# Layer 0 of a hybrid decoder step: the exponential's series and S5's input tables move from DVE to POOL, and POOL's larger memsets move behind its loads

## What is computed

```python
proj = jnp.einsum('btd,de->bte', x, w_in)
o_hg, s_hg_new = _chunked_gated_linear(...)      # HGRN2
o_rt, s_rt_new = _chunked_gated_linear(...)      # retention
y5, s_re_new, s_im_new = _s5_scan(su, s5_log_dt, s5_a_re, s5_a_im, s5_b_re, s5_b_im, ...)
mixed = jnp.concatenate([o_hg, o_rt, y5], axis=-1) @ w_out
x = _layer_norm(ALPHA * x + mixed, ln1_w, ln1_b)
ff = jnp.square(jax.nn.relu(x @ w_up)) @ w_down
x = _layer_norm(ALPHA * x + ff, ln2_w, ln2_b)
```

## Time and profile before

| | |
|---|---|
| median of 3 runs | 835.95 us (834.85 to 836.22) |
| the profiled execution | 836.35 us |
| its span, first to last instruction | 834.6 us |
| PE busy | 749.3 us (90%), 7662 matmuls |
| DVE busy | 577.6 us (69%), 1056 instructions |
| ACT busy | 416.0 us (50%), 760 instructions |
| POOL busy | 36.0 us (4%), 44 instructions |
| mean granted PE clock | 0.948 of 2.4 GHz |

### The profile page before, as it was taken

How to read it: one execution, slowest core, us unless ns; L and a number is a source line. 1 busy time by engine, 2 the same in 40 slices (tenths; PEclk the granted TensorE clock), 3 DMA queues, 4 the chain that set the end, 5 groups by cost and what they waited for, 6 DMA issues and landing times. The chain is left out here.

```text
span 834.6 us, 18462 instructions
## 1 busy us (share of the span) xinstructions
PE 749.3 (90%) x7662; PEld 711.0 (85%) x7662; DVE 577.6 (69%) x1056; ACT 416.0 (50%) x760; POOL 36.0 (4%) x44
## 2 busy tenths in 40 slices
PE   4779678988999999989997989799899999999994
PEld 4669667788999999989986988587799999999993
DVE  7997995445778899885445789834577886666443
ACT  4726131444577755446345624444466874455323
POOL 4000010210000000000010002010000000000000
PEclk9989886998999999999996999899899999999998
DMA  8442111352435455444441333413144555555521
GB/s 330 150 143 85 53 53 50 114 203 74 141 123 179 167 177 192 159 145 142 173 152 51 102 104 105 143 51 110 55 173 139 184 172 187 178 177 178 179 99 53
DMA packets 30580, 113.61 MB, mean 136 GB/s; under 512 B 3521, under 2 KB 3729, under 8 KB 29985
## 3 DMA queue, kind: packets, MB, share of 16 engines
q1 hardware_dynamic: 27936, 101.83, 36.6%
q0 software_dynamic: 1984, 9.52, 3.0%
q10 hardware_dynamic: 576, 1.08, 0.3%
HBM read 108.24 MB, written 4.18 MB: 135 GB/s over the span
## 5 line engine op out<-in xcount | busy, mean ns | idle before, releaser
L1436 DVE TENSOR_TENSOR w_low<-w_raw,w_high 128x1024 fp32r<-128x1024 f32 x192 | 236.5, 1232 | 152.3 <-ACT w_high L1014 149.6
L1014 ACT ACTIVATE w_high<-w_raw 128x1024 fp32r<-128x1024 f32 x192 | 202.5, 1055 | 242.6 <-PE stream L963 231.5
L961 PE MATMUL stream<-a_high,w_high 128*128 128x264 f32 x768 | 237.9, 310 | 33.7 <-DVE a_low L1441 21.7
L962 PE MATMUL stream<-a_low,w_high 128*128 128x264 f32 x768 | 229.2, 298 | 0.0
L963 PE MATMUL stream<-a_high,w_low 128*128 128x264 f32 x768 | 228.4, 297 | 0.0
L961 PEld LDWEIGHTS stream<-a_high,w_high 128*128 128x128 f32 x768 | 155.8, 203 | 44.3 <-issue 22.4
L962 PEld LDWEIGHTS stream<-a_low,w_high 128*128 128x128 f32 x768 | 156.3, 204 | 0.3
L963 PEld LDWEIGHTS stream<-a_high,w_low 128*128 128x128 f32 x768 | 155.7, 203 | 0.0
L961 PE MATMUL stream<-h_high,w_high 128*128 128x264 f32 x512 | 148.6, 290 | 1.2 <-issue 0.5
L962 PE MATMUL stream<-h_low,w_high 128*128 128x264 f32 x512 | 145.1, 283 | 0.0
L963 PE MATMUL stream<-h_high,w_low 128*128 128x264 f32 x512 | 145.0, 283 | 0.0
(11 more groups left out here) (369 smaller groups left out, 953.7 us busy)
## 6 DMA issues: line engine op xcount, KB each, us to landing
w_raw<-in_weights SPq DMA_DIRECT2D x192, 512.0 KB, 3.3
mats<-in_matrices POOLq DMA_DIRECT2D x2, 1024.0 KB, 5.5
S_hg<-in_state_hg POOLq DMA_DIRECT2D x2, 768.0 KB, 5.0
out_hg_s<-S_hg POOLq DMA_DIRECT2D x2, 768.0 KB, 3.7
consts<-in_constants POOLq DMA_DIRECT2D x1, 1484.5 KB, 9.2
X<-in_xT ACTq DMA_DIRECT2D x4, 264.0 KB, 5.7
out_y<-X SPq DMA_DIRECT2D x1, 1056.0 KB, 3.9
S_rt<-in_state_rt POOLq DMA_DIRECT2D x2, 512.0 KB, 7.1
```

The source lines that it names most:

```text
L961: pe.matmul(bnk[:, 0:width], wh, xh, start=(first and kk == 0), stop=False)
L962: pe.matmul(bnk[:, 0:width], wh, xl, start=False, stop=False)
L1014: act.activation(w_high[:, n % SPLIT_SLOTS, :], w_raw[:, n % RAW_SLOTS, :], ACT.Copy).then_inc(high_ready, 1)
L1436: put(tt(w_low[:, n % SPLIT_SLOTS, :], w_raw[:, n % RAW_SLOTS, :], w_high[:, n % SPLIT_SLOTS, :].bitcast(F32), ALU.subtract), low_ready)
```

## The change

Three things change in layer 0; layer 1 is left as it was.

1. POOL evaluates the series and the squarings (`magnitudes`, 21 instructions of 128x8) right after it has cleared two of the five tiles. DVE waits for `mag_ready` instead. The piece with the complex value is now run before the loop. By the new `PIECES` all that iteration 7 had finished before is finished there again, but for the second half of the fourth output step (L1545, L1546), which comes in iteration 8.
2. POOL makes the input tables (`input_powers`, one copy and twelve tensor_tensor), after the loads of the states. It waits for S5's matrices, for the complex value (`turn_power_ready`) and for ACT's `s5_rot`. Its two temporaries lie in the memory of `V_tok`. PE's `s5_tab_in` waits for `powin_ready`.
3. The three larger clearings of POOL come behind its loads of the constants. `s5_rot` is moved from ACT's iteration 4 to iteration 3.

```diff
 WIDE = T + 2
-PIECES = (2, 3, 3, 2, 2, 2, 2, 2, 2)
+PIECES = (2, 2, 2, 2, 2, 2, 2, 2)
 TABLE_STEPS = len(PIECES)
 FIRST_UNITS = 10
-ROT_AT = 4
+ROT_AT = 3
 _plan(10, *[("s5_tab_in", 0, _t) for _t in range(4)], layers=(0,))
...
         pow_ready = sem("pow_ready")
+        powin_ready = sem("powin_ready")
+        pool_step = sem("pool_step")
+        mag_ready = sem("mag_ready")
+        turn_power_ready = sem("turn_power_ready")
         tab_ready = sem("tab_ready")
...
+        DT, RC, RS_, COS, SIN, TH, ZR, EX, MAG, ABR, ABI, DEN, GR, GI, T0, T1, T2, PC, PS, NR = range(20)
+        def row(i):
+            return par[:, i, :]
+        def wide(i, shape):
+            return row(i).unsqueeze(1).unsqueeze(3).broadcast_to(shape)
         block = ctx.enter_context(nc.Block())
...
+            steps = {"n": 0}
+            def then(ins, s=None):
+                if s is None:
+                    steps["n"] += 1
+                    ins.then_inc(pool_step, 1)
+                    pool.wait_ge(pool_step, steps["n"])
+                else:
+                    ins.then_inc(s, 1)
+            def magnitudes():
+                tt, ts = pool.tensor_tensor, pool.tensor_scalar
+                pool.wait_ge(vecs_loaded, 16)
+                pool.wait_ge(act_params, 1)
+                then(tt(row(ZR), row(DT), pv(0, "a_re"), ALU.mult))
+                then(ts(row(ZR), row(ZR), 1.0 / 16, None, ALU.mult))
+                then(ts(row(EX), row(ZR), 1.0 / 8, 1.0, ALU.mult, ALU.add))
+                for n in range(7, 0, -1):
+                    then(tt(row(EX), row(EX), row(ZR), ALU.mult))
+                    then(ts(row(EX), row(EX), 1.0 / n, 1.0, ALU.mult, ALU.add))
+                for n in range(3):
+                    then(tt(row(EX), row(EX), row(EX), ALU.mult))
+                then(tt(row(MAG), row(EX), row(EX), ALU.mult), mag_ready)
+            def input_powers():
+                tt = pool.tensor_tensor
+                both = [128, 2, 8, 32]
+                t0, t1 = (tab_tmp[1][:, 512 * i:512 * i + 512].rearrange("p (r j c) -> p r j c", r=2, j=8) for i in range(2))
+                powers = s5_pow_in[0]
+                pool.wait_ge(mats_loaded, 16)
+                pool.wait_ge(turn_power_ready, 1)
+                pool.wait_ge(rot_ready, 1)
+                then(pool.tensor_copy(powers[:, :, :, S5_STEP - 1, :], BT_s5))
+                for i in range(S5_STEP - 1, 0, -1):
+                    src, dst = powers[:, :, :, i, :], powers[:, :, :, i - 1, :]
+                    then(tt(t0, src, wide(ABR, both), ALU.mult))
+                    then(tt(t1, src, wide(ABI, both), ALU.mult))
+                    then(tt(dst[:, 0, :, :], t0[:, 0, :, :], t1[:, 1, :, :], ALU.subtract))
+                    then(tt(dst[:, 1, :, :], t0[:, 1, :, :], t1[:, 0, :, :], ALU.add), powin_ready if i == 1 else None)
             a, n = CV["steps"]
...
             pool.memset(near_packed[:, :, :, :], 0.0).then_inc(cleared, 1)
-            pool.memset(near[:, :, :, :, :], 0.0).then_inc(cleared, 1)
-            pool.memset(st_p[:, :, :], 0.0).then_inc(cleared, 1)
-            pool.memset(level_space, 0.0).then_inc(cleared, 1)
+            magnitudes()
             pool.wait_ge(x_loaded[1], 16)
...
             pool.dma_start(s5x0[:, :, :, :, :], state_s5).then_inc(const_loaded, 16)
+            pool.memset(near[:, :, :, :, :], 0.0).then_inc(cleared, 1)
+            pool.memset(st_p[:, :, :], 0.0).then_inc(cleared, 1)
+            pool.memset(level_space, 0.0).then_inc(cleared, 1)
             for l in range(DEPTH):
...
                     load_states(0)
+                    input_powers()
                 else:
...
                 if t == 0:
-                    pe.wait_ge(pow_ready, 2 * lx + 2)
+                    pe.wait_ge(powin_ready, lx + 1)
                 b = unit(l, u)
...
                 lx, h = u[1:]
-                pe.wait_ge(pow_ready, 2 * lx + 1)
+                pe.wait_ge(pow_ready, lx + 1)
                 b = unit(l, u)
...
-            DT, RC, RS_, COS, SIN, TH, ZR, EX, MAG, ABR, ABI, DEN, GR, GI, T0, T1, T2, PC, PS, NR = range(20)
-            def row(i):
-                return par[:, i, :]
             def split_low(n):
...
-                chain(tt(row(ZR), row(DT), are, ALU.mult))
-                chain(ts(row(ZR), row(ZR), 1.0 / 16, None, ALU.mult))
-                chain(ts(row(EX), row(ZR), 1.0 / 8, 1.0, ALU.mult, ALU.add))
-                for n in range(7, 0, -1):
-                    chain(tt(row(EX), row(EX), row(ZR), ALU.mult))
-                    chain(ts(row(EX), row(EX), 1.0 / n, 1.0, ALU.mult, ALU.add))
-                yield
-                for n in range(4):
-                    chain(tt(row(MAG if n == 3 else EX), row(EX), row(EX), ALU.mult))
+                if l:
+                    chain(tt(row(ZR), row(DT), are, ALU.mult))
+                    chain(ts(row(ZR), row(ZR), 1.0 / 16, None, ALU.mult))
+                    chain(ts(row(EX), row(ZR), 1.0 / 8, 1.0, ALU.mult, ALU.add))
+                    for n in range(7, 0, -1):
+                        chain(tt(row(EX), row(EX), row(ZR), ALU.mult))
+                        chain(ts(row(EX), row(EX), 1.0 / n, 1.0, ALU.mult, ALU.add))
+                    yield
+                    for n in range(4):
+                        chain(tt(row(MAG if n == 3 else EX), row(EX), row(EX), ALU.mult))
+                else:
+                    dve.wait_ge(mag_ready, 1)
                 dve.wait_ge(act_params, 2 * l + 2)
                 chain(tt(row(ABR), row(MAG), row(COS), ALU.mult))
-                chain(tt(row(ABI), row(MAG), row(SIN), ALU.mult))
+                chain(tt(row(ABI), row(MAG), row(SIN), ALU.mult), turn_power_ready)
                 chain(ts(row(NR), row(ABR), -1.0, None, ALU.add))
...
-                def wide(i, shape):
-                    return row(i).unsqueeze(1).unsqueeze(3).broadcast_to(shape)
                 both, one = [128, 2, 8, 32], [128, 8, 32]
...
+                if l == 0:
+                    settle()
+                    dve.sem_inc(table_ready, 1)
+                    return
                 dve.wait_ge(rot_ready, l + 1)
...
                     put(tt(dst[:, 0, :, :], t0[:, 0, :, :], t1[:, 1, :, :], ALU.subtract))
-                    chain(tt(dst[:, 1, :, :], t0[:, 1, :, :], t1[:, 0, :, :], ALU.add), pow_ready if i == 1 else None)
+                    chain(tt(dst[:, 1, :, :], t0[:, 1, :, :], t1[:, 0, :, :], ALU.add), powin_ready if i == 1 else None)
                     if i == 1:
```

## The result

| | before | changed |
|---|---|---|
| median | 836.48 us (834.85 to 840.47, 8 runs) | 842.61 us (840.19 to 844.45, 8 runs) |
| ratio of the two | | 1.0053, 95% interval 1.0032 to 1.0074 |
| the profiled execution, its span | 836.35, 834.6 us | 844.45, 842.7 us |
| PE busy, DVE busy | 749.3, 577.6 us | 757.7, 576.1 us |
| POOL busy, instructions | 36.0 us, 44 | 57.2 us, 78 |

The kernel is 0.3 to 0.7% slower. The point that the prediction called decisive, the start of `level_decay(0)` on DVE, moved from 53.50 to 58.55 us. That is 5.05 us later, where the sum had said 5.8.

What follows compares the result with a forecast made beforehand. DVE sets the pace until 57 us, PE after it; the start of level_decay(0) decides. 8.1 − 4.2 − 0.5 − 9.2 = −5.8 us, so slower: 841.8 us as a median, range 832 to 849.

Steps and rivals of the forecast that it cites:

- saved: blocked pair, series, squarings, output step: DVE ahead of level_decay(0): 2.9 us from the blocked pair, 3.6 series, 0.8 squarings, 0.8 output step; 8.1 us saved.
- wait for the magnitude: Early layer 0: DVE waits 4.2 us (0 to 12) for POOL's 21 operations, begun after a 4.9 us code load.
- clearings' stall: POOL's moved memsets, about 18.8 to 23.2 us, may hold a DVE tensor_scalar: 0.5 us lost, 0 to 2.7.
- sine tables ahead of the split of chunk 6: On ACT, tables end at 34.4 and the split at 35.4, about when DVE wants it: cost 0.
- POOL's reads beside DVE: From 34.4 us to level_decay(0), POOL's thirteen table operations take turns with DVE's: 9.2 us lost, lower bound 4.8.
- The input tables save nothing: Their thirteen DVE operations lie behind level_decay(0), under PE's full stretch, with 3.82 us over: removing them gains 0.
- No turns: Rival: POOL's arithmetic does not hold DVE; only the magnitude wait is left; 3.4 us faster, 828 to 834; 18 in 100.
- Late POOL: Rival: code load takes 9.8 us, magnitude wait 9, tables cost DVE 11; 848.4 us, 845 to 850; 21 in 100.
- the two middle terms: DVE's wait for the magnitude, 4.2 us, and the stall under POOL's moved memsets, 0.5 us.
- chain without air: From 57 us on, first PE then DVE work without slack, so lateness at its head arrives late at the end.

Runs made afterwards that it cites:

- the control: The kernel before, unchanged, measured and traced once more: 837.05 us, ratio 1.0005.
- the tables alone: The kernel before with only layer 0's input tables moved to POOL; series, memsets and sine tables as before: 847.28 us, ratio 1.0094.
- −2.8 for the memsets: The kernel before with its three large memsets behind the state loads and sine tables, and the sine tables one chunk later (`ROT_AT = 5`): 834.58 us, ratio 0.9967.
- the best one: The changed kernel with input tables back on DVE, the three large memsets behind the sine tables, and `ROT_AT = 5`: 832.30 us, ratio 0.992.
- the memsets late with the series on POOL and `ROT_AT = 4`: The changed kernel with input tables back on DVE, the three large memsets behind the sine tables, and `ROT_AT = 4`: 834.25 us, ratio 0.9965.

## Why the prediction was right, and what in it was wrong

The time, the sign, the place and the leading mechanism were right. Its sum for the decisive point was 5.8 us later; measured, 5.05. But of its terms two were far off and one was left out, and that the sum came out is in good part luck. By terms:

| term | predicted | measured | shown by |
|---|---|---|---|
| saved: blocked pair, series, squarings, output step | 8.1 | 8.1 | with the memsets later, DVE's first output step starts at 29.66, before at 36.77: 7.1, and 0.2 of wait and 0.8 of output step make 8.1; in the changed kernel it starts at 33.11, with 3.4 lost to the memsets |
| wait for the magnitude | 4.2 | 0.2 | L1529 at 12.62, POOL done at 12.58 |
| clearings' stall | 0.5 | 3.4 | L2056, 3.80 for 0.37 us; undone, the point is 3.2 earlier |
| sine tables ahead of the split of chunk 6 | 0 | 1.75 | idle row at 36.27; undone, 0.9 at the point; with the memsets later, 0.87 |
| POOL's reads beside DVE | 9.2 | 7.8 | twelve operations of DVE; undone 7.1, with 0.9 of new wait; alone 8.2 |
| sum | −5.8 | −5.05 | −5.05 in the trace |

- *Added: DVE waits for the magnitude.* The step failed at its first number, 4.9 us for a load of code, taken from a transfer of 32 KB. POOL's first operation came 1.0 us behind its configuration and waited for ACT. The Trainium skill (GPSIMD Engine Reference, Instruction dispatch) speaks of about 6 us at the first call into freshly loaded code. In this trace there is no such gap: 1.0 us, with the wait for ACT in it. The other number of the step was right: its 21 operations take from 4.34 to 12.58 us, 8.2 where 8.4 were worked out, though by another split, 0.29 us for an operation alone, 0.35 beside DVE, and over 1 us for the two beside DVE's splits of weights (L515 at 7.54 and L519 at 11.52).
- *Moved: the clearings.* The mechanism was named, the place was missed, and for a reason that lies in the term before: with POOL 4 us earlier than assumed, the memsets fell on the two tensor_scalars on the bounds instead of behind them. The prediction had kept 2.7 us as this term's end, one memset. Three in a row did 3.4.
- *Moved: the sine tables.* The prediction itself said that if DVE were earlier, ACT would be the wait. What it had not seen is that ACT's split of chunk 5 waits for its weights until 28.40, so that ACT could not be early. In the changed kernel:

```profile
28.40 1.06 ACT L1071 ACTIVATE w_high<-w_raw 128x1024 fp32r<-128x1024 f32 x1 [9.59 <-DMA w_raw<-in_weights]
...
34.16 1.06 ACT L1084 ACTIVATE rot<-scratch 128x1024 f32<-128x1024 f32 x1
35.13 1.04 ACT L1071 ACTIVATE w_high<-w_raw 128x1024 fp32r<-128x1024 f32 x1
```

  Half of the 1.75 us, too, comes from the memsets. SP may load chunk 5 only when DVE's `w_low` of chunk 2 is done, and the stall had pushed that from 17.1 to 20.5 us. With the memsets behind the sine tables the same split of ACT starts 4.3 us earlier, and DVE's idle time ahead of chunk 6 is 0.87 us. The load itself takes longer as well: in the kernel before it was issued at 21.87 and the split started at 26.30, in the changed kernel at 20.55 and 28.40. POOL's loads now stand right ahead of it; that this slows it is not shown. The variant's timeline of ACT:

```profile
24.07 1.06 ACT L1072 ACTIVATE w_high<-w_raw 128x1024 fp32r<-128x1024 f32 x1 [5.48 <-DMA w_raw<-in_weights]
```

- *Added: POOL reads SBUF beside a full DVE.* The largest term, and the best: 1.04 to 1.11 us for POOL's undisturbed 512-column operations where the affine_select gave 1.08, and turns at nearly each. It was 1.4 us too high; DVE lost little to some of them (0.4 us by w_low at 44.05).
- *The input tables save nothing.* Right: left out altogether, the time stays.
- *Rivals.* "No turns" rested on L1447 beside the memset of `near`. That row was right and did not bear on the question, as the memsets in place of the tables show: a memset does not read. "Late POOL" rested on a load of code that did not come.

The errors of the two middle terms, 4.0 us too dear and 2.9 too cheap, hang together: they are one wrong start of POOL, read at two places. That is why their sum was good; with a tensor_tensor in place of the pair at 15.5 us the second error would not have been there to meet the first. The other two errors, 1.75 us too cheap and 1.4 too dear, have no common cause: that they cancel is luck.

From the point to the end: 5.05 us became 6.1 by the medians, and 4.4 by the ratio (2.7 to 6.2). But the 5.1 us do not arrive whole, as the prediction's chain without air would have it. By DVE's splits the lateness is 5.1 us at chunk 10, 2.3 at chunk 12 and 3.4 at chunk 15. At chunk 12 the kernel before is itself held, by its input tables on DVE; its split comes at 64.78, right behind them. Chunk 15 follows PE. Part of what is missing there is the clock: in the trace of before PE's granted clock is lower from 56 to 64 us than in the changed kernel's (the windows below are of before, then of the changed kernel). Against the control, which has its half-speed stretches elsewhere, the lateness at chunk 15 is 3.8. How much of the rest is air in the chain, and how much the clock, no run separates. What comes back and goes again behind that lies within what the clock does from run to run. Over the variants the two numbers go together (+8.2 and +7.9 us for the tables alone, −2.9 and −2.8 for the memsets, −7.0 and −6.7 for the best one, each by its ratio), save three: input tables back on DVE, the memsets late with the series on POOL and `ROT_AT = 4`, and the changed kernel with `ROT_AT = 4`. Their ends are 3 to 4 us above their points. The first and the last have a lower mean granted clock (0.940 and 0.939, before 0.946), but so have the changed kernel (0.940) and the tables alone (0.941), whose ends fit their points; and the second has 0.947. So the clock does not explain it, and it stays open.

```profile
56.00:60.00 4.00, 2.94 (x14) 2.63 (x13) 3.75 (x8) 0.00 (x0) 0.00 (x0) 0.50 0.41 135
60.00:64.00 4.00, 4.00 (x82) 3.74 (x82) 3.90 (x8) 1.34 (x2) 0.00 (x0) 0.70 0.38 131
```

```profile
56.00:60.00 4.00, 4.00 (x100) 3.86 (x100) 3.62 (x9) 0.61 (x1) 0.00 (x0) 0.70 0.37 131
60.00:64.00 4.00, 2.13 (x76) 1.89 (x67) 3.51 (x5) 0.72 (x2) 0.00 (x0) 1.00 0.41 135
```

## What to carry to other kernels

Work that is moved to POOL to free DVE cost DVE next to nothing here where it was small, or where it only wrote; where it read SBUF beside two-input operations of DVE, both engines lost, and DVE lost 8 us for thirteen operations that it could have done hidden under PE. Ask of each piece that is moved what its old place had cost: the series stood on the path and was worth moving, the input tables did not. A long POOL memset has to be placed with an eye on the one kind of DVE instruction that it was seen to stop here, the tensor_scalar, and a moved engine start shifts every such meeting behind it. A stall on DVE is paid twice where a load waits for DVE: here 3.4 us on DVE itself and 0.9 us through the late load of chunk 5.

## What was not expected of the hardware

- A tensor_scalar of DVE stands behind a POOL memset down to the smallest size: two of 3 columns took 3.80 us for 0.37, one of 256 columns 2.60 for 0.28, while tensor_tensors beside the same memsets kept their 0.16 us. Three memsets in a row that do not wait for each other held the pair to the end of the last. Among the twelve chained ones of 1024 columns, which wait for each other, a tensor_scalar of 256 columns took its usual 0.28 us, at 38.20, about where the first memset ended and the second began.
- POOL's arithmetic started without any visible load of code: two records of 45 ns of configuration, and the first operation 1.0 us later, 0.15 us after ACT's step sizes were done.
- A POOL tensor_tensor of 8 columns takes 0.20 us by its record and 0.29 by the distance of starts; DVE's chained step is 0.20 to 0.21.
- One kernel's executions differ by 4 us at 155 us and by 0.1 at the end of the profile, with the half-speed stretches of PE's granted clock at other places.
